# A third weight unit in the head of a hybrid decoder layer, and multiplies of a matrix of ones on TensorE

## The reference

```python
mod = silu(c) @ w_ada + b_ada
sh1, sc1, gt1, sh2, sc2, gt2 = split(mod, 6)
h = rmsnorm(x, norm1_g) * (1 + sc1) + sh1
xr, gr, q, k, v, o, ig, fg, u = split(h @ w_in)
xc = causal_dwconv(xr); y_a = rglru(xc) * gelu(gr)        # a, i gates are two matmuls of xc
y_b = sigmoid(o) * rmsnorm(mlstm(q, k, v, ig, fg))        # chunks of 128 tokens
y_c = pool_mix(u)
x = x + gt1 * (concat(y_a, y_b, y_c) @ w_out)
h2 = rmsnorm(x, norm2_g) * (1 + sc2) + sh2
x = x + gt2 * (square(relu(h2 @ w_ff1)) @ w_ff2)
y = rmsnorm(x, final_g)
```

## Time and profile before

| | us |
|---|---|
| median of 3 runs | 1166.48 (1163.81 to 1166.8) |
| the profiled execution, its own time | 1164.52 |
| its span | 1162.7 |
| TensorE busy in the span | 1116.7 (96%) |
| VectorE busy | 798.7 (69%) |
| ScalarE busy | 468.2 (40%) |
| GpSimd busy | 343.4 (30%) |
| mean granted TensorE clock, of full speed | 0.989 |

### The profile page before, as it was taken

The page is one execution under the profiler, slowest core; times in us unless marked ns, Lnnn a source line. Parts: engine busy times, 40 slices in busy tenths (PEclk is TensorE's granted clock), DMA queues, the critical chain, the costliest instruction groups (busy, mean ns, idle before and its releaser), DMA issues.

```text
span 1162.7 us, 19579 instructions
## 1 busy us (share of the span) xinstructions
PE 1116.7 (96%) x7205; PEld 1070.1 (92%) x7205; DVE 798.7 (69%) x1318; ACT 468.2 (40%) x766; POOL 343.4 (30%) x273
## 2 busy tenths in 40 slices
...
GB/s 342 306 58 144 113 91 128 233 157 230 120 110 134 246 73 73 37 57 36 40 34 58 70 19 74 56 16 72 72 18 72 54 22 86 36 54 55 37 1 146
DMA packets 76037, 109.85 MB, mean 94 GB/s; under 512 B 6434, under 2 KB 58950, under 8 KB 75590
## 3 DMA queue, kind: packets, MB, share of 16 engines
...
...
## 4 chain that ended last, share of the span: by engine, by line
PE 77%; DVE 13%; DMA 4%; ACT 3%; issue 1%; POOL 1%; SPq 1%; ACTq 0%; POOLq 0%; DVEq 0%
PE D L2459 6%; PE D L2643 6%; PE D L2645 6%; PE D L2644 6%; PE D L2461 5%; PE D L2460 5%; PE X L2645 5%; PE X L2643 5%; PE X L2644 5%; PE X L2715 5%; PE X L2717 5%; PE X L2716 5%; PE D L2715 2%; PE D L2717 2%; PE D L2716 2%; DMA SPARE<-in_WADA 2%
## 5 line engine op out<-in xcount | busy, mean ns | idle before, releaser
L2459 PE MATMUL D<-H_hi,W_hi 128*128 128x344 f32 x472 | 158.7, 336 | 4.7 <-POOL H_lo L1120 3.9
L2461 PE MATMUL D<-H_hi,W_lo 128*128 128x344 f32 x472 | 152.1, 322 | 0.0
L2460 PE MATMUL D<-H_lo,W_hi 128*128 128x344 f32 x472 | 152.0, 322 | 0.0
L1120 POOL TENSOR_TENSOR Y_lo<-FU,Y_hi 128x344 fp32r<-128x344 f32 (+3 forms) x84 | 100.2, 1196 | 153.7 <-ACT Y_hi L1556 87.5
L1115 POOL TENSOR_TENSOR W_lo<-RAWW,W_hi 128x1024 fp32r<-128x1024 f32 x25 | 61.4, 2458 | 179.9 <-ACT W_hi L1269 179.6
L2459 PEld LDWEIGHTS D<-H_hi,W_hi 128*128 128x128 f32 x472 | 90.2, 191 | 15.3 <-issue 9.5
L1120 POOL TENSOR_TENSOR Y_lo<-EY,Y_hi 128x344 fp32r<-128x344 f32 (+1 forms) x24 | 38.4, 1599 | 216.3 <-ACT Y_hi L1556 144.5
L2460 PEld LDWEIGHTS D<-H_lo,W_hi 128*128 128x128 f32 x472 | 90.1, 191 | 0.6 <-issue 0.2
L2461 PEld LDWEIGHTS D<-H_hi,W_lo 128*128 128x128 f32 x472 | 89.8, 190 | 0.0
L2261 DVE SCALAR_TENSOR_TENSOR X<-X,MOD 128x344 f32<-128x344 f32 (+1 forms) x138 | 75.7, 567 | 9.2 <-PE X L2717 9.1
L2715 PE MATMUL X<-Y_hi,W_hi 128*128 128x344 f32 x252 | 80.7, 320 | 0.0
...
## 6 DMA issues: line engine op xcount, KB each, us to landing
...
X0T<-in_x SPq DMA_DIRECT2D x3, 1376.0 KB, 12.0
...
```

What stands on the lines that cost most here:

```text
L1120: nc.gpsimd.tensor_tensor(lo_v, fu_v, hi_v.bitcast(F32), ALU.subtract).then_inc(lo_ready, 1)
L2459: T.matmul(out, w_h, hi[:, kt, a:b], start=(kt == 0), stop=False)
L2460: T.matmul(out, w_h, lo[:, kt, a:b], start=False, stop=False)
L2461: one = T.matmul(out, w_l, hi[:, kt, a:b], start=False, stop=(kt == KT - 1))
```

## The change

There are two parts. Unit 2 (xr0) joins units 0 and 1: its weights are loaded right behind the 16th piece, split by ScalarE and VectorE into two buffers of their own (`W2_hi`, `W2_lo`), and its words become `DK` words beside those of units 0 and 1. The unit xr0 is written to another place (`XR[0]`), which the gate buffer `TH` overlaps, so `OUTC` is copied from it ahead of the convolution. `V:0` and `V:2` are cut in two (`VK` and `V`), with `NS` between. The words from `D:2:2` to `D:6:2` are arranged anew. Second, TensorE multiplies the matrix of ones by itself, 128 columns, into bank D2: 30 times at the start, 8 times once x of chunk 0 is there, and twice behind each `ADA` word that a `PW:2` follows, of which the list has eleven, 60 multiplies in all.

```diff
+WARM_FIRST, WARM_NEXT = 30, 8
-SP_AFTER = {5: ("w0",), 7: ("w1",), 15: ("wv", "x1"), 17: ("x2",), 18: ("w2",)}
+SP_AFTER = {5: ("w0",), 7: ("w1",), 15: ("w2", "wv", "x1"), 17: ("x2",)}
-N_DVE_W = 2
+N_DVE_W = 3
+N_FIRST = 3
 MIX_ORDER = """
-SQ:0:0 SQ:0:1 ADA:0:0 ADA:0:1 ADA:4:0 ADT:0 ADM:0 NS:0 ADA:4:1 ADA:1:0 ADT:4 ADM:4 ADA:1:1 W:0 N:0:0 N:0:1 WL:0
-ADA:5:0 ADT:1 ADM:1 ADA:5:1 ADT:5 ADM:5 W:1 DK:0:0:0:1 ADA:2:0 N:0:2 N:0:3 DK:0:0:1:2 ADA:2:1 WL:1 ADA:6:0 ADT:2 ADM:2 DK:1:0:0:2
-    ADA:6:1 DK:0:0:2:4 ADT:6 ADM:6 ADA:3:0 ADA:3:1 N:0:4 N:0:5 DK:1:0:2:4 ADA:7:0 ADT:3 ADM:3 ADA:7:1 ADT:7 ADM:7 N:0:6 N:0:7
+SQ:0:0 SQ:0:1 ADA:0:0 PW:2 ADA:0:1 PW:2 ADA:4:0 PW:2 ADT:0 ADM:0 NS:0 ADA:4:1 PW:2 ADA:1:0 PW:2 ADT:4 ADM:4 ADA:1:1 PW:2 W:0 N:0:0 N:0:1 WL:0
+ADA:5:0 PW:2 ADT:1 ADM:1 ADA:5:1 PW:2 ADT:5 ADM:5 W:1 DK:0:0:0:1 ADA:2:0 PW:2 N:0:2 N:0:3 DK:0:0:1:2 ADA:2:1 PW:2 WL:1 ADA:6:0 PW:2 ADT:2 ADM:2 DK:1:0:0:2
+    ADA:6:1 DK:0:0:2:4 ADT:6 ADM:6 ADA:3:0 ADA:3:1 N:0:4 N:0:5 DK:1:0:2:4 ADA:7:0 ADT:3 ADM:3 ADA:7:1 ADT:7 ADM:7 W:2 N:0:6 N:0:7 WL:2
 DK:0:0:4:6 DK:1:0:4:6 WV:0 DK:0:0:6:7
 WV:1 DK:1:0:6:7
 WV:2 DK:0:0:7:8
-WV:3 DK:1:0:7:8
+WV:3 DK:1:0:7:8 DK:2:0:0:8
 D:0:0 SQ:1:0
-D:1:0 SQ:1:1 V:0 NS:1 ADA:8:0 N:1:0 N:1:1 V:1 N:1:2 N:1:3 DK:0:1:0:1
-DK:1:1:0:1
+D:1:0 SQ:1:1
+D:2:0 VK:0:0:5 NS:1 V:0 ADA:8:0 N:1:0 N:1:1 V:1 N:1:2 N:1:3 DK:0:1:0:1
+DK:1:1:0:1 DK:2:1:0:1
...
-DK:1:1:7:8
+DK:1:1:7:8 DK:2:1:7:8
 D:0:1
-D:1:1 V:2 NS:2 N:2:8 N:2:0 R:13 N:2:1 N:2:2 V:3 N:2:3 N:2:4 N:2:5 N:2:6 V:4 N:2:7 DK:0:2:0:8
-W:2 V:5
+D:1:1
+D:2:1 VK:2:0:4 NS:2 V:2 N:2:8 N:2:0 R:13 N:2:1 N:2:2 V:3 N:2:3 N:2:4 N:2:5 N:2:6 V:4 N:2:7 DK:0:2:0:8 V:5
 D:0:2 R:14 DK:1:2:0:8
 ADA:8:2 ADA:8:3 R:15 V:6 V:7 W:3 V:8 R:17 ADT:8
-D:1:2 ADM:8 ADA:9:0 G1 ADA:9:1
-D:2:0 R:16
-D:2:1 R:18 G2
-D:2:2 R:20 W:4 G3 ADA:9:2 R:19 R:21
-D:3:0 ADA:9:3 G4
-D:3:1 R:23 ADT:9 LRUC:0
-D:3:2 ADM:9 W:5 ADA:10:0
-D:4:0 R:22 ADA:10:1 LRUG:0 R:24 LRUA:0
-D:4:1 LRUM:0
-D:4:2 R:26 W:6
-D:5:0 ADA:10:2 ADA:10:3 R:25 LRUC:1
-D:5:1
-D:5:2 ADT:10 R:27 ADM:10 ADA:11:0 LRUG:1 ADA:11:1
-D:6:0 R:29 W:7 LRUA:1 R:28 R:30
-D:6:1 LRUM:1
-D:6:2 R:32 ADA:11:2
+D:1:2 ADM:8 ADA:9:0 G1 ADA:9:1 DK:2:2:0:8
+D:2:2 R:16
+D:3:0 R:18 G2
+D:3:1 R:20 W:4 G3 ADA:9:2 R:19 R:21
+D:3:2 ADA:9:3 G4
+D:4:0 R:23 ADT:9 LRUC:0 ADM:9 W:5
+D:4:1 ADA:10:0 R:22 ADA:10:1
+D:4:2 LRUG:0 R:24 LRUA:0
+D:5:0 LRUM:0 R:26 W:6
+D:5:1 ADA:10:2 ADA:10:3 R:25
+D:5:2 LRUC:1 ADT:10 R:27 ADM:10 ADA:11:0
+D:6:0 LRUG:1 ADA:11:1 R:29 W:7
+D:6:1 LRUA:1 R:28 R:30
+D:6:2 LRUM:1 R:32 ADA:11:2
 D:7:0
 D:7:1 W:8 ADA:11:3 LRUC:2 R:31
 D:7:2 ADT:11 LRUG:2 LRUA:2
...
-    return ((2 * c + u) % NCH, (2 * c + u) // NCH) if u < 2 else (c, u)
+    return (u, c) if u < N_FIRST else (c, u)
...
+            def warm(n):
+                for _ in range(n):
+                    T.matmul(DB[NCH - 1][:, 0:P], ONE[:], ONE[:], start=True, stop=True)
+            pe.wait_ge(ones_ready, 7)
+            warm(WARM_FIRST)
+            pe.wait_ge(ld_x[0], 16)
+            warm(WARM_NEXT)
```

More of the change, by code:

```diff
@@ L103 @@
 WV:2 DK:0:0:7:8
-WV:3 DK:1:0:7:8
+WV:3 DK:1:0:7:8 DK:2:0:0:8
 D:0:0 SQ:1:0
-D:1:0 SQ:1:1 V:0 NS:1 ADA:8:0 N:1:0 N:1:1 V:1 N:1:2 N:1:3 DK:0:1:0:1
-DK:1:1:0:1
+D:1:0 SQ:1:1
+D:2:0 VK:0:0:5 NS:1 V:0 ADA:8:0 N:1:0 N:1:1 V:1 N:1:2 N:1:3 DK:0:1:0:1
+DK:1:1:0:1 DK:2:1:0:1
 N:1:4 DK:0:1:1:2
-DK:1:1:1:2
+DK:1:1:1:2 DK:2:1:1:2
 N:1:5 DK:0:1:2:3
-DK:1:1:2:3
+DK:1:1:2:3 DK:2:1:2:3
 N:1:6 DK:0:1:3:4
-DK:1:1:3:4
+DK:1:1:3:4 DK:2:1:3:4
 N:1:7 DK:0:1:4:5
-DK:1:1:4:5
+DK:1:1:4:5 DK:2:1:4:5
 R:12 ADA:8:1 DK:0:1:5:6
-SQ:2:0 DK:1:1:5:6
+SQ:2:0 DK:1:1:5:6 DK:2:1:5:6
 DK:0:1:6:7
-DK:1:1:6:7
+DK:1:1:6:7 DK:2:1:6:7
 SQ:2:1 DK:0:1:7:8
-DK:1:1:7:8
+DK:1:1:7:8 DK:2:1:7:8
 D:0:1
-D:1:1 V:2 NS:2 N:2:8 N:2:0 R:13 N:2:1 N:2:2 V:3 N:2:3 N:2:4 N:2:5 N:2:6 V:4 N:2:7 DK:0:2:0:8
-W:2 V:5
+D:1:1
+D:2:1 VK:2:0:4 NS:2 V:2 N:2:8 N:2:0 R:13 N:2:1 N:2:2 V:3 N:2:3 N:2:4 N:2:5 N:2:6 V:4 N:2:7 DK:0:2:0:8 V:5
 D:0:2 R:14 DK:1:2:0:8
 ADA:8:2 ADA:8:3 R:15 V:6 V:7 W:3 V:8 R:17 ADT:8
-D:1:2 ADM:8 ADA:9:0 G1 ADA:9:1
-D:2:0 R:16
-D:2:1 R:18 G2
-D:2:2 R:20 W:4 G3 ADA:9:2 R:19 R:21
-D:3:0 ADA:9:3 G4
-D:3:1 R:23 ADT:9 LRUC:0
-D:3:2 ADM:9 W:5 ADA:10:0
-D:4:0 R:22 ADA:10:1 LRUG:0 R:24 LRUA:0
-D:4:1 LRUM:0
-D:4:2 R:26 W:6
-D:5:0 ADA:10:2 ADA:10:3 R:25 LRUC:1
-D:5:1
-D:5:2 ADT:10 R:27 ADM:10 ADA:11:0 LRUG:1 ADA:11:1
-D:6:0 R:29 W:7 LRUA:1 R:28 R:30
-D:6:1 LRUM:1
-D:6:2 R:32 ADA:11:2
+D:1:2 ADM:8 ADA:9:0 G1 ADA:9:1 DK:2:2:0:8
[12 more added lines that the diff above has]
+D:6:2 LRUM:1 R:32 ADA:11:2
 D:7:0
@@ L361, in build @@
         WV_hi = at("WV_hi", [P, KT, VCOLS], slot[8], F32R)
-        XR = [at(f"XR{t}", [P, SEQ + CONV - 1], slot[3 + t]) for t in range(3)]
+        XR = [at(f"XR{t}", [P, SEQ + CONV - 1], slot[3 + t] if t else slot[13] + 96) for t in range(3)]
+        W2_hi, W2_lo = at("W2_hi", [P, KT * P], slot[11] + 160, F32R), at("W2_lo", [P, KT * P], slot[12] + 128, F32R)
         XC, RG = at("XC", [P, TOK], slot[6]), at("RG", [P, TOK], slot[7])
@@ L1319, in _ @@
                     if s[1] < N_EARLY_W:
-                        w_hi(s[1], None, s[1] % 2, None)
+                        if s[1] == N_FIRST - 1:
+                            act.wait_ge(w_lo_ready, N_FIRST - 1)
+                        w_hi(s[1], None, s[1] % 2, None, to=W2_hi if s[1] == N_FIRST - 1 else None)
                     else:
@@ L1818, in _ @@
                     dve.wait_ge(w_hi_ready, u + 1)
-                    V.tensor_tensor(W_lo[:, u, :], WR[u][:], W_hi[:, u, :].bitcast(F32), ALU.subtract).then_inc(w_lo_ready, 1)
+                    w_h, w_l = (W2_hi[:], W2_lo[:]) if u == N_FIRST - 1 else (W_hi[:, u, :], W_lo[:, u, :])
+                    V.tensor_tensor(w_l, WR[u][:], w_h.bitcast(F32), ALU.subtract).then_inc(w_lo_ready, 1)
                 elif k == "WV":
@@ L1880, in _ @@
                         dve.wait_ge(d_free[c], unit_of("xr", t) + 1)
+                    link(V.tensor_copy(OUTC[:, t, :], XR[t][:, SEQ:]))
                     w = lambda j: col("conv_w", t * CONV + j)
@@ L1892, in _ @@
                             tell(last, xc_ready, t + 1)
-                    link(V.tensor_copy(OUTC[:, t, :], XR[t][:, SEQ:]))
                 elif k == "LRUA":
```

27 lines of the change are left out of this document (18 added, 9 removed).

## The result

The changed kernel takes 1173.85 us (median of 9 runs, 1172.1 to 1178.56), the kernel before 1166.87 us beside it (9 runs, 1163.81 to 1169.81): a ratio of 1.0062 with a 95% interval of 1.0045 to 1.0079, so 7 us **slower**. Forecast were 1168.9 us and at most 1172.5.

What follows compares the result with a forecast made beforehand. TensorE, busy 96% of the span, bounds the kernel, behind a load, then the LRU chain. -4.9 + 7.8 + (26.3 - 25.5) - (30.25 - 29.0) = +2.4 us on the median 1166.48 gives 1168.9, range 1161.5 to 1172.5.

Steps and rivals of the forecast that it cites:

- the sum of +2.4 us: Whole kernel: head gain, later `LRUG:0` and both LRU stretches together make `LRUG:2` 2.4 us later, carried to the end.
- The head gains 4.9 us: Head: unit 2 joining units 0 and 1 fills TensorE's idle and gains 4.9 us, bounds 3.5 and 6.1.
- the lag at the last early piece: Head: TensorE ready late for the piece landing at 34.1 us; 0.3 taken, up to 2 in the bounds.
- two other places: LRU stretches: VectorE stalled beside GpSimd's `W_lo`, 2.4 us in the first and 2.31 in the second.
- What the new order does to the LRU chain: LRU stretches: less cover, so `LRUG:1` 26.3 us behind `LRUG:0`, `LRUG:2` 29.0 later; TensorE waits 4.7 and 3.8.
- Rival 1: New LRU waits: the clock falls, 1.7 us a fall, +4.1 or +5.8, 1170.6 to 1172.3 us; chance 0.24.
- 3.8 is over 3.7: Argument for the clock falling: the new 3.8 us wait exceeds the 3.72 us idle that was followed by a fall.
- Multiplies of ones at 0: Start: faster pieces gain nothing because a load ends this stretch; cost 0, bounds 0 and +2 us.
- Behind it the two lists agree and all is timed from TensorE: Behind `LRUG:2`: its 2.4 us delay carries unchanged to the end.
- The range: Whole kernel: 1161.5 to 1172.5 us, from the head gain holding without its end to both clock falls.

Runs made afterwards that it cites:

- wl2_wv0: Changed kernel with only `WL:2` moved, behind `WV:0` on VectorE: 1173.20 us, ratio 1.0050 to the kernel before.
- lru_cover: Changed kernel with `LRUG:1` one D word later, `LRUG:2` two later, `LRUM:2` ahead of `SMA TS TSD`: 1172.68 us, ratio 1.0040.
- order_alone: Kernel before, head untouched, with only the LRU words and loads between `D:4:0` and `D:6:2` moved as in the change (`LRUC:0` stays): 1178.19 us, ratio 1.0093.
- w6_early: Changed kernel with `W:6` ahead of `LRUG:0` and `R:25` behind `LRUA:0`: 1171.86 us, ratio 1.0042 to the kernel before.
- head_fix: Changed kernel with `WL:2` behind `WV:3` and without the pairs of ones (the first 38 stay): 1179.49 us, ratio 1.0113.
- no_ones: Changed kernel without any of the multiplies of ones: 1174.21 us, ratio 1.0055 to the kernel before.
- ones_in_waits: Changed kernel plus multiplies of ones in TensorE's two new waits, 10 ahead of `ADA:11:0`, 11 ahead of `LRUG:2`: 1169.82 us, ratio 1.0021.
- ones_only: Kernel before plus the 60 multiplies of ones, nothing else: 1167.65 us, ratio 0.9996.
- both_fix: head_fix with `W:6` also ahead of `LRUG:0` and `W:8` behind `LRUC:2`, against the changed kernel: 1174.75 us, ratio 1.0072.
- g2_late: w6_early with `LRUG:2` and `LRUA:2` also moved behind `D:8:0`: 1167.73 us, ratio 1.0011 to the kernel before.

## Why the prediction was wrong

Set against the trace, the sum of +2.4 us fell 8.0 short of the 10.4 in the span: 3.2 in the head, 1.0 in the two stretches (0.35 and 0.68), 2.6 in `LRUG:2` itself, and 1.1 behind it. These are readings of one execution of each kernel.

- **"The head gains 4.9 us"**: this step failed. `LRUG:0` was to come at 141.5 and came at 144.73, a gain of 7.8 - 6.15 = 1.65, outside the bounds given (3.5 to 6.1). Of the 3.2 us missing, 0.9 are the lag at the last early piece (35.33 against 34.4), which had been allowed for in the bounds: from the first piece to the last early one it took 23.65 us and not 21.8, because the 22 multiplies of ones took some 6.5 us there and not 5.1. Another 0.4 lie between `NS:1` and `LRUG:0` (92.9 against 92.5). The other 1.9 lie between the last early piece and `NS:1` (16.46 against 14.6). The text put `WL:2` into VectorE's 1.33 us idle as free. But that idle is the time in which GpSimd makes the last two `H_lo` tiles, and both engines were asked for at once: the tiles took 3.50 us instead of 1.81, TensorE idled 2.31 and then ran at half clock for 2.7 us (43.06 to 45.78). VectorE's `WV_lo` was held as well, 5.03 us instead of the 4.22 given. The prediction priced this contention in two other places and not in this one. wl2_wv0 bears out 1.3 of the 1.9; the other 0.6 stays open.
- **"What the new order does to the LRU chain"**: this held. `LRUG:1` was given 26.3 us and took 26.65, `LRUG:2` 29.0 and 29.68; `W_lo` of `W:6` was put 14.75 us behind `LRUG:0` and is 14.65 behind, with a stall of 2.1 where 2.4 stood. One wait was shown under another name: the last releaser in the first stretch is the load `R:25`, which the text had not seen. It ends with the same `W_lo`, so the time is the same, but lru_cover, which moved `LRUG:1` and not the load, could not remove it. order_alone shows the loss of this step by itself.
- **Rival 1, "The clock falls at the new waits"**: it came, at both, and should have stood in the sum. Its price of 1.7 us a fall was mis-sized for `LRUG:2`, which lost 2.6 here. The price was taken from the windows of 332 to 336 us, but the clock was still at 0.50 up to 338 (336.00:338.00, in the rows of the kernel before), so that fall was longer than the 3.4 us counted. In other executions the price was about right: `LRUG:2` lost 1.4 to 1.7 us in order_alone, w6_early, head_fix and wl2_wv0 (5.14 to 5.43 us behind idles of 3.07 to 3.30), and nothing in no_ones. The fall at `D:6:0` costs little in the changed kernel, because `XC` ends no earlier (170.95): in ones_in_waits `LRUG:1` follows 26.28 us behind `LRUG:0` instead of 26.65, `LRUG:2` 28.83 behind that instead of 29.68, and runs in 3.74. "3.8 is over 3.7" was no guide: the clock fell behind idles of 2.31, 3.03 and 3.33 us, and in the kernel before behind one of 0.56.
- **Multiplies of ones at 0**: right in the time (ones_only, 0.9996), within its interval. The first piece came at 11.68, a little under the 12.0 to 15.0 given. The reason was not quite right: at the last early piece TensorE was late and no load. They may take away a risk, since in no_ones, head_fix and both_fix the pieces were slow for longer, but no time shows it by itself.
- **"Behind it the two lists agree and all is timed from TensorE"**: in the lists, yes, but the clock does not repeat. Both traces wait some 1.45 us for `EX`, at 233.85 and, in the kernel before, at 224.46. Behind it the changed kernel's clock is 0.50 from 234 to 240 us and the D word takes 6.2 us instead of 4.0. The kernel before falls 9 us behind that place, at its two waits for loads (1.17 and 1.32). At 267.40 the changed kernel waits 1.57 us for `EX` where before waits 0.59, and its clock falls once more. What is left of these swings is 1.1 us. No run tested how much of it belongs to the change; g2_late, otherwise at before's time, has a slow D word there too (5.6).
- **The range** (to 1172.5) ended at both falls on top of a head that gains 4.9. It lacked the case in which the head's gain and the clock fail together, and that is the one that came.
